# Late expert rows added by identity products in PSUM at the end of a streaming encoder step

## The reference, cut to what matters

```python
def _moe_swiglu(h, w_router, b_router, w_exp_in, w_exp_out):
    ...
    out = jnp.zeros_like(h)
    for e in range(N_EXPERTS):
        out = out + combine[..., e:e + 1] * _swiglu(h, w_exp_in[e], w_exp_out[e])
    return out
...
    f = _moe_swiglu(h, ...)
    x = x + gate_f * f
y = _rmsnorm(x, p["g_final"])        # x * rsqrt(mean(x*x) + eps) * g_final
```

## Time and profile before

| | us |
|---|---|
| median of three executions | 1411.81 |
| lowest and highest | 1409.66, 1411.97 |
| the profiled execution, its own time | 1410.49 |
| its span, first to last instruction | 1408.5 |
| PE busy (share of the span) | 1360.9 (97%) |
| DVE busy | 1024.4 (73%) |
| ACT busy | 793.0 (56%) |

### The profile page before, as it was taken

One profiled execution on the slowest core, in us unless ns is written; L12 is line 12 of the kernel. 1 busy time (PEld: TensorE's weight loads), 2 busy tenths in 40 slices (PEclk: granted clock), 3 DMA queues, 4 the chain that ended last, 5 costly groups with the idle time before them and its releaser, 6 DMA issues.

```text
span 1408.5 us, 25176 instructions
## 1 busy us (share of the span) xinstructions
PE 1360.9 (97%) x9653; PEld 1214.9 (86%) x9653; DVE 1024.4 (73%) x1416; ACT 793.0 (56%) x1088; POOL 42.9 (3%) x66
## 2 busy tenths in 40 slices
PE   5999999999899999999999999998999999999997
PEld 4889999878899999997999998787688888888885
DVE  2477999887554444245689998875798988898887
ACT  2534348736453333235444487364777787788764
POOL 0010100000000000000001000000200000000020
PEclk9899999999999999999999999999999999999999
DMA  9957744225746867636578762254999999999994
GB/s 332 241 170 226 240 143 131 66 85 178 204 122 193 260 193 236 218 120 182 152 235 270 208 198 92 76 179 161 271 363 384 377 386 383 377 386 386 374 382 145
DMA packets 282693, 328.43 MB, mean 233 GB/s; under 512 B 34654, under 2 KB 192806, under 8 KB 282598
## 3 DMA queue, kind: packets, MB, share of 16 engines
q1 hardware_dynamic: 276146, 317.18, 68.5%
q0 software_dynamic: 1472, 5.24, 1.5%
q10 hardware_dynamic: 4980, 4.69, 1.0%
HBM read 312.41 MB, written 14.66 MB: 232 GB/s over the span
## 4 chain that ended last, share of the span: by engine, by line
PE 85%; DVE 7%; DMA 2%; ACT 2%; issue 2%; SPq 0%; DVEq 0%; ACTq 0%
PE mmp L941 15%; PE mmp L943 14%; PE mmp L942 14%; PE mmp L1460 8%; PE mmp L1461 8%; PE mmp L1459 8%; PE mmp L935 4%; DVE conv L2231 2%; PE px L1024 2%; DMA more<-in_w_exp_out_dram 1%; PE px L1225 1%; DMA ring<-in_w_out_dram 1%; PE lg L1024 1%; DVE ring_lo L2399 1%; PE lg L1181 1%
## 5 line engine op out<-in xcount | busy, mean ns | idle before, releaser
L941 PE MATMUL mmp<-hT_hi,wm_hi 128*128 128x320 f32 (+1 forms) x976 | 311.0, 319 | 5.8 <-issue 3.1
L943 PE MATMUL mmp<-hT_hi,ring_lo 128*128 128x320 f32 (+1 forms) x976 | 303.2, 311 | 0.0
L942 PE MATMUL mmp<-hT_lo,wm_hi 128*128 128x320 f32 (+1 forms) x912 | 282.0, 309 | 0.0
L2142 DVE TENSOR_TENSOR ring_lo<-ring,wm_hi 128x1024 fp32r<-128x1024 f32 (+1 forms) x124 | 148.3, 1201 | 67.5 <-ACT wm_hi L1693 65.1
L941 PEld LDWEIGHTS mmp<-hT_hi,wm_hi 128*128 128x128 f32 (+1 forms) x976 | 183.8, 188 | 10.2 <-issue 7.9
L943 PEld LDWEIGHTS mmp<-hT_hi,ring_lo 128*128 128x128 f32 (+1 forms) x976 | 183.9, 188 | 0.2
L1693 ACT CAST wm_hi<-ring 128x1024 fp32r<-128x1024 f32 (+1 forms) x124 | 126.8, 1031 | 81.2 <-PE mmp L943 74.9
L942 PEld LDWEIGHTS mmp<-hT_lo,wm_hi 128*128 128x128 f32 (+1 forms) x912 | 172.0, 189 | 0.4
L2399 DVE TENSOR_TENSOR more_lo<-more,we_hi_a 128x2048 fp32r<-128x2048 f32 (+2 forms) x64 | 128.1, 2020 | 15.6 <-ACT we_hi_a L1889 15.5
L1630 ACT ACTIVATE tmp<-mmp 128x320 f32<-128x320 f32 x68 | 29.7, 437 | 188.9 <-PE mmp L943 154.9
L2231 DVE SCALAR_TENSOR_TENSOR conv<-u_conf,dwc,conv 128x350 f32<-128x350 f32 x240 | 132.1, 581 | 3.1
(11 more groups left out here) (414 smaller groups left out, 2874.9 us busy)
## 6 DMA issues: line engine op xcount, KB each, us to landing
ring<-in_w_in_dram SPq DMA_DIRECT2D x104, 512.0 KB, 4.9
ring<-in_w_exp_in_dram SPq DMA_DIRECT2D x64, 512.0 KB, 7.5
more<-in_w_exp_in_dram SPq DMA_DIRECT2D x64, 512.0 KB, 11.3
ring<-in_w_ada_dram SPq DMA_DIRECT2D x52, 512.0 KB, 7.4
more<-in_w_exp_out_dram SPq DMA_DIRECT2D x48, 512.0 KB, 6.0
wide<-in_w_ada_dram SPq DMA_DIRECT2D x44, 512.0 KB, 7.4
ring<-in_w_ffn_in_dram SPq DMA_DIRECT2D x44, 512.0 KB, 5.5
ring<-in_w_branch_dram SPq DMA_DIRECT2D x48, 256.0 KB, 2.9
```

The costliest lines, as they stand in the source:

```text
L941: nc.tensor.matmul(out, w_hi, x_hi, start=is_first, stop=False)
L942: nc.tensor.matmul(out, w_hi, x_lo, start=False, stop=False)
L943: return nc.tensor.matmul(out, w_lo, x_hi, start=False, stop=is_last)
L2142: V.tensor_tensor(mix_rows(ring_lo, l, s, r), mix_rows(ring, l, s, r), mix_hi(l, s, r).bitcast(F32), ALU.subtract).then_inc(mix_lo_ready, 1)
```

## The change: what it does

The late rows are no longer added by VectorE. TensorE adds them: two products of 512 columns for each t with the identity as the stationary side and `late[t]` as the moving one go into `z_banks(t)`, between the residual's products and the scattered rows'. So `add_z` falls away with its semaphore, ScalarE squares `z_banks(t)` itself and writes the unused squares into `y_late[t]`, and the last scaling reads `z_banks(t)`. `gate_late(t)` now releases a semaphore for TensorE. TensorE's order changes as well: residual and late rows of t=0 and t=1 come first, then the scattered rows of both, then t=2.

```diff
                     run_pass(last, True)
                     pe.wait_ge(szT_ready, 1)
-                    for t in range(3):
-                        if t == 2:
-                            pe.wait_ge(y_gated_ready, 3)
+                    def kept_rows(t):
                         for c in range(DC):
                             nc.tensor.matmul(z_banks(t)[0:rows[t], c * P:(c + 1) * P],
                                              xT[:, c, t * P:t * P + rows[t]], ident[:], start=(c % 4 == 0), stop=False)
+                        pe.wait_ge(late_gated, t + 1)
+                        for h in range(2):
+                            c = slice(h * 512, (h + 1) * 512)
+                            nc.tensor.matmul(z_banks(t)[0:rows[t], c], ident[0:rows[t], 0:rows[t]],
+                                             late[t][0:rows[t], c], start=False, stop=False)
+
+                    def last_rows(t):
                         for h in range(2):
                             if t == 0:
                                 pe.wait_ge(y_gated_ready, h + 1)
...
                         ins.then_inc(z_done, 1)
+
+                    kept_rows(0)
+                    kept_rows(1)
+                    last_rows(0)
+                    last_rows(1)
+                    pe.wait_ge(y_gated_ready, 3)
+                    kept_rows(2)
+                    last_rows(2)
...
-                        act.wait_ge(z_added, t + 1)
-                        nc.scalar.activation(z_banks(t)[0:m, :], y_late[0:m, t, :], ACT.Square,
+                        act.wait_ge(z_done, t + 1)
+                        nc.scalar.activation(y_late[0:m, t, :], z_banks(t)[0:m, :], ACT.Square,
                                              accum_out=sum_sq[0:m, t, :]).then_inc(z_squared, 1)
...
-                        link(V.tensor_tensor(late[t][0:m], late[t][0:m], gate_rows[t // 2][0:m, :], ALU.mult))
+                        V.tensor_tensor(late[t][0:m], late[t][0:m], gate_rows[t // 2][0:m, :],
+                                        ALU.mult).then_inc(late_gated, 1)
...
-                    def add_z(t):
-                        m = P if t < 2 else TS
-                        dve.wait_ge(z_done, t + 1)
-                        V.tensor_tensor(y_late[0:m, t, :], z_banks(t)[0:m, :], late[t][0:m],
-                                        ALU.add).then_inc(z_added, 1)
-
...
-                        V.scalar_tensor_tensor(x_tok[0:m, t, :], y_late[0:m, t, :], r_root[0:m, t, :], fin_row[0:m, :],
+                        V.scalar_tensor_tensor(x_tok[0:m, t, :], z_banks(t)[0:m, :], r_root[0:m, t, :], fin_row[0:m, :],
                                                ALU.mult, ALU.mult).then_inc(out_ready, 1)
...
                     join_late(2)
-                    add_z(0)
                     gate_late(2)
                     dve.wait_ge(fin_loaded, 16)
-                    end_row(0)
-                    add_z(1)
-                    add_z(2)
-                    end_row(1)
-                    end_row(2)
+                    for t in range(3):
+                        end_row(t)
```

More of the change, by code:

```diff
@@ L536, in build @@
         z_done = sem("z_done")
-        z_added = sem("z_added")
+        late_gated = sem("late_gated")
         z_squared = sem("z_squared")
```

## The result

The changed kernel takes 1413.84 us (median of 20 runs, 1409.09 to 1417.12) and the kernel before 1410.99 (20 runs, 1406.51 to 1413.81). The ratio is 1.0022, with a 95% interval of 1.0014 to 1.0031: 3.1 us slower by the ratio, 2.85 us by the medians.

The account below looks back on a forecast made before the run. TensorE's last groups, then a serial chain, were taken to bound the end. Products add 5.16 us, the closed gap returns 0.78, the removed sum 1.26: 3.11 us later, 1414.9 us (ratio 1.0022), range 1411.8 to 1416.4.

Parts of the forecast that it names:

- TensorE sets the end: In the last 20 us the chain runs through TensorE's last groups, so product time added there delays the end.
- products that cost nothing: Limiting case for a gain: free identity products would leave -2.05 us, under 0.2%; a gain beyond that got 0.04.
- the span should be 1411.6: Sign to check in the changed kernel's profile: the whole execution's span in us.
- The price of the products: Six float32 identity products on TensorE, 12 records at 0.43 us each, add 5.16 us.
- The rival of cheap products: Identity products run at 0.23 us a record, 2.40 us less, 1412.5 us, no change that could be told; chance 0.10.
- The gap: TensorE's pause before the second half of t=0's scattered rows, waiting for VectorE's gating, closes and returns 0.78 us.
- The sum removed: VectorE's sum of t=2 leaves the path between TensorE's end and the square: 1.29 less 0.03 handover, 1.26 us.
- The waits for `late_gated`: TensorE's new waits for gated late rows cost nothing; the smallest margin is 2.4 us.
- Reading from and writing to PSUM: Square and last scaling of t=2 now read PSUM; both edits cost 0.00 us, upper end 0.15.
- The sum on TensorE: TensorE's groups from first residual product to end total 16.04 us, ending 4.37 us later than before.
- The quicker last store: Rival: the last store no longer waits behind the one before, returning up to 0.38 us, 1414.5 us; chance 0.22.
- The sign: Slower by more than 0.2% (2.82 us), since 3.11 us stands just outside; slower 0.56, same 0.40, faster 0.04.

Follow-up runs that it names:

- e1: The changed kernel without its six identity products, all waits kept; stretch (first residual product to end of span) 17.12 us, ratio to before 0.9978.
- e2: The changed kernel with each identity product issued twice; stretch 27.72 us, ratio to before 1.0058.
- e5: The changed kernel with identity products in the rounded float32 type, late rows losing low bits; stretch 18.73 us, ratio to before 0.9996.
- e3: The kernel before with TensorE's new order but no identity products, VectorE keeping its three sums; stretch 18.96 us, ratio to before 1.0007.
- e4: The changed kernel with TensorE's groups in the old order, products and all else kept; stretch 22.53 us, ratio to before 1.0019.
- e7: The changed kernel with identity products for t=0 and t=1 only, VectorE adding t=2 as before; stretch 21.86 us, ratio to before 1.0015.
- e9b: The changed kernel with late rows of t=2 at full height, 64 rows cleared, stationary side 128x64; stretch 22.29 us, ratio to before 1.0023.
- e10b: The changed kernel with rounded identity products, residual products of t=0 in the last pass, late rows of t=2 at full height; ratio to before 0.9994.

## Why the prediction was right, point by point

*TensorE sets the end.* Right. e1 and e2 move the stretch by -5.44 and +5.16 us for 12 records less and more, and in the changed kernel TensorE runs from its first residual product to its end without a mark. With the products gone the stretch is 2.12 us shorter than before; the prediction had -2.05 for products that cost nothing. Its sign "the span should be 1411.6" did not come true (1414.0), because the program ahead of the changed part took 2.2 us longer in that execution; the stretch, which leaves this out, is the fair comparison.

*The price of the products.* Right: 0.43 us a record was taken, and 1.71, 1.72 and 1.85 us a group were measured, 5.28 in all against 5.16. The rival of cheap products needs the rounded type; e5 gave it, with a stretch 3.83 us shorter than the changed kernel's, against the rival's 2.40, which left out that a rounded product is one record instead of two.

*The gap.* Right that it closes, but it was worth 0.88 us and not 0.78. The scattered rows of t=0 took 2.60 us before (1391.05 to 1393.65), and take 1.71 in the changed kernel and 1.72 in e3. The prediction put 0.10 of the 0.96 us behind the wait down to a step from 512-column to 128-column work, and kept it in its sum as the 1.81 us of the late rows of t=0. They took 1.71, directly ahead of 128-column work, and e4 has 1.72 at the very place; so the 0.10 belonged to the wait and went with it. The closing is not the new order's doing either: e4 shows that the products alone do it.

*The sum removed.* Right: 1.29 us less the handover, which by the timeline is 0.04 us from TensorE to ScalarE, so 1.25 where 1.26 was put. e7 puts the sum back and pays 1.31 us for it.

*The waits for `late_gated`.* Right, none is seen. The smallest margin in the changed kernel is that of t=0, gated at 1390.81 and wanted at 1393.23: 2.4 us.

*Reading from and writing to PSUM.* Right at 0.00 for the scaling; the square gained 0.04 us. The groups of the square and of the last scaling in the changed kernel, by form (mean ns):

```profile
L2036 ACT ACTIVATE y_late<-mmp 128x1024 f32<-128x1024 f32 x1 | 1.0, 1025 | 0.2 <-PE mmp L1532 0.2
L2644 DVE SCALAR_TENSOR_TENSOR tok<-mmp,small,more 128x1024 f32<-128x1024 f32 x1 | 1.3, 1284 | 0.0
```

They took 1027 and 1284 ns with `y_late` as input. By these lengths the square is as long as before, but what comes behind it starts earlier. Its sum is read out 0.92 us after its start and 0.96 us before, by ScalarE's timelines of t=2, before and changed:

```profile
1402.22 1.02 ACT L2023 ACTIVATE mmp<-y_late 64x1024 f32<-64x1024 f32 x1 [0.18 <-DVE y_late L2629]
1403.18 0.19 ACT L2023 ACTIVATION_READ_ACCUMULATOR mmp<-y_late 64x1 f32 x1
...
1407.69 1.02 ACT L2036 ACTIVATE y_late<-mmp 64x1024 f32<-64x1024 f32 x1 [4.17 <-PE mmp L1532]
1408.61 0.19 ACT L2036 ACTIVATION_READ_ACCUMULATOR y_late<-mmp 64x1 f32 x1
```

e7, where this square reads SBUF again, has 0.96 (1406.90 to 1407.86). An estimate from the table on the Trainium skill's page "VectorE: DVE Perf Modes" (section on the TRN2 errata) has the scaling 0.065 us longer from PSUM and the square 0.043 shorter. For ScalarE the traces agree; for VectorE they do not, with 1284 ns from either source in instructions of 1024 columns.

*The sum on TensorE.* 16.04 us were predicted and 16.21 measured. The term that was mis-sized is t=2, of which the prediction said that its 64 rows change nothing: its groups were put at 1.80, 1.72 and 1.88 us and took 1.90, 1.85 and 1.93, 0.28 more; the other groups took 0.11 less than put, 0.10 of it the late rows of t=0 (see the gap). The whole stretch grew by 3.32 us instead of 3.11.

*The quicker last store.* This rival did not come true. The last store of the changed kernel, by SP's timeline and its DMA:

```profile
1410.65 0.54 SPq L834 DMA_DIRECT2D out_dram<-tok  x1
...
out_dram<-tok SPq DMA_DIRECT2D x1, 256.0 KB, 2.9
```

Its data move from 1411.8 on, again 1.15 us after the issue began, though the store before it had been issued 5.6 us earlier. The 0.38 us are the store's own and were no wait.

*The sign.* It rested on 3.1 us against a bound of 2.8, and the measured ratio stands at the same place, 1.0022, its interval reaching below 1.002. That the change is slower is measured; that it is slower by over 0.2% is only likely. That the ratio agrees in its fourth digit is luck: its interval is 2.4 us wide, and the terms that were off by 0.28 and 0.11 us partly cancel.

## What to carry to other kernels

Moving a sum to the accumulating engine pays only if that engine has room at that very place; compare what is added to its path with what leaves the path, here 5.3 us against 1.3 for the sum and 0.9 for the gap. An identity product in float32 costs 0.86 us for 512 columns, a VectorE sum 1.22 for 1024; in the rounded type it is 0.28, and only then is it the cheaper of the two. Where runs scatter by 0.2% and the change by as much, measure the stretch from the last point that both kernels share.

## What the runs showed of the hardware

A float32 group with a stationary side of 64x64 and 64 moving rows between groups of 128x64 costs 0.28 us more than the same work at 128x64 with 128 moving rows: 0.10 in the group before, 0.13 in its own and 0.05 behind (e9b). It is paid once a group (e2). The weight loads show where it comes from. The first of t=2, in the changed kernel and in e9b:

```profile
1403.86 0.19 PEld L1524 LDWEIGHTS mmp<-more,ident 64*64 64x64 f32 x2 [0.17 <-issue]
```

```profile
1401.43 0.25 PEld L1528 LDWEIGHTS mmp<-y_late,ident 128*64 128x64 f32 x2
```

In the changed kernel the product starts at 1403.87, together with the load; in e9b it starts at 1401.54, 0.11 us behind it. There the load was done ahead, as it is for the groups of t=0 and t=1, whose first loads start at 1393.12 and 1396.62 for products at 1393.23 and 1396.73. The same is seen where the residual of t=2 goes over from a side of 128x128 to one of 128x64: its first load starts with its product, at 1401.97 in the changed kernel and 1397.25 before, and the group ahead takes 1.81 us instead of 1.72:

```profile
1401.97 1.72 PEld L1519 LDWEIGHTS mmp<-ident,xT 128*64 128x64 f32 x16 [0.76 <-issue]
```

So in float32, at each of the three changes of the side's shape in these traces, the first load is not done ahead and about 0.1 us is lost; no run varied the shape alone. It is not the whole rule either. A rounded group of 128x64 between float32 groups of 128x64 also starts together with its first load (both at 1399.77, e10b). The residual, this group and the last one take 1.89, 0.60 and 1.93 us there. At 128x128 the residual and the rounded group of t=1 take 1.70 and 0.55 us (e5), and a last group without such a neighbour takes 1.88 (e1): 0.29 us less in all. Why is open.

TensorE's granted clock was 1.00 (2.4 GHz) over its whole 16.21 us and 0.50 (1.2 GHz) while the data of the last store moved, as before.
